# A fused two-stage network on one core: block 1's attention and scan woven into its projections, heads in pairs

## What is computed

```python
u = rmsnorm(x, ln1_g)
q, k, v, pool_in, z, xbc, dt_raw, gate_pre = split(u @ w_in)
y_a = dilated_attention_mixer(q, k, v, rel_bias) @ w_a   # 3 groups of 6 heads, 64 features, dilation 1, 4, 16
y_b = pool_mixer(pool_in, pool_w, pool_scale) @ w_b      # windows 2, 4, 8, 16
y_c = ssd_mixer(z, xbc, dt_raw, ...) @ w_c               # conv + silu, scan in 4 chunks of 128, gate by silu(z), norm
g = sigmoid(gate_pre + b_gate)
x = x + (g[0] * y_a + g[1] * y_b + g[2] * y_c) @ w_o
x = x + conv_ffn(rmsnorm(x, ln2_g), ...)
```

## Time and profile before

| | |
|---|---|
| Median of 3 runs | 3329.92 us (3324.21 to 3331.27) |
| The profiled execution | 3329.93 us, span 3328.1 us |
| PE busy | 3144.7 us (94%), 13268 instructions |
| PE weight loads | 2424.1 us |
| DVE busy | 1571.3 us (47%) |
| ACT busy | 1248.2 us (38%) |
| Granted PE clock, mean | 0.956 of 2.4 GHz |
| Transfers | 259.04 MB, mean 78 GB/s |

### The profile page before, as it was taken

How to read it: one execution, slowest core, us unless ns; L and a number is a source line. 1 busy time by engine, 2 the same in 40 slices (tenths; PEclk the granted TensorE clock), 3 DMA queues, 4 the chain that set the end, 5 groups by cost and what they waited for, 6 DMA issues and landing times. The chain is left out here.

```text
span 3328.1 us, 36122 instructions
## 1 busy us (share of the span) xinstructions
PE 3144.7 (94%) x13268; PEld 2424.1 (73%) x13268; DVE 1571.3 (47%) x2141; ACT 1248.2 (38%) x1848; POOL 392.7 (12%) x233
## 2 busy tenths in 40 slices
PE   7888899979999999889999999999989999999998
PEld 6777678747777877556667788888656667788887
DVE  3323463664376466654553354143654554354241
ACT  3323232414254244454444343133554453342231
POOL 4000000000000000101111122222101111122221
PEclk9677899989999999999999999999999999999999
DMA  6111233202232333212222233333212222233332
GB/s 171 39 51 50 59 88 84 83 1 70 83 107 85 100 94 95 57 32 64 70 71 70 70 95 99 97 95 109 62 39 64 70 71 70 76 95 98 98 95 89
DMA packets 460161, 259.04 MB, mean 78 GB/s; under 512 B 20202, under 2 KB 452172, under 8 KB 460016
## 3 DMA queue, kind: packets, MB, share of 16 engines
q1 hardware_dynamic: 454064, 246.03, 25.6%
q0 software_dynamic: 5952, 11.13, 1.2%
HBM read 254.98 MB, written 5.64 MB: 78 GB/s over the span
## 5 line engine op out<-in xcount | busy, mean ns | idle before, releaser
L657 ACT ACTIVATE wH<-wR 128x1024 fp32r<-128x1024 f32 (+1 forms) x476 | 491.3, 1032 | 494.7 <-DMA wR<-in_w_mlp_out_dram 197.5
L662 DVE TENSOR_TENSOR wL<-wR,wH 128x1024 fp32r<-128x1024 f32 (+1 forms) x332 | 395.9, 1193 | 582.6 <-ACT wH L657 570.8
L693 POOL TENSOR_TENSOR wL<-wR,wH 128x1024 fp32r<-128x1024 f32 (+1 forms) x144 | 346.0, 2403 | 2002.1 <-ACT wH L657 2002.1
L712 PE MATMUL ps<-uH,wH 128*128 128x512 f32 x1224 | 485.3, 396 | 15.7 <-DVE wL L662 12.7
L712 PE MATMUL ps<-uL,wH 128*128 128x512 f32 x1224 | 480.0, 392 | 0.0
L712 PE MATMUL ps<-uH,wL 128*128 128x512 f32 x1224 | 479.5, 392 | 0.0
L724 PE MATMUL ps<-uH,wH 128*128 128x512 f32 x928 | 381.7, 411 | 5.0 <-DVE wL L662 3.6
L724 PE MATMUL ps<-uL,wH 128*128 128x512 f32 x928 | 379.5, 409 | 0.0
L724 PE MATMUL ps<-uH,wL 128*128 128x512 f32 x928 | 376.6, 406 | 0.0
L712 PEld LDWEIGHTS ps<-uH,wH 128*128 128x128 f32 x1224 | 232.3, 190 | 74.1 <-DVE wL L662 22.6
L712 PE MATMUL ps<-mH,wH 128*128 128x512 f32 x688 | 267.9, 389 | 2.1 <-DVE wL L662 2.1
(11 more groups left out here) (441 smaller groups left out, 4476.4 us busy)
## 6 DMA issues: line engine op xcount, KB each, us to landing
wR<-in_w_in_dram SPq DMA_DIRECT2D x185, 512.0 KB, 3.7
wR<-in_w_mlp_in_dram SPq DMA_DIRECT2D x64, 512.0 KB, 4.0
wR<-in_w_mlp_out_dram SPq DMA_DIRECT2D x64, 512.0 KB, 4.0
wR<-in_ffn_w_up_dram SPq DMA_DIRECT2D x44, 512.0 KB, 3.7
wR<-in_w_branch_dram SPq DMA_DIRECT2D x24, 512.0 KB, 3.4
wR<-in_w_out_dram SPq DMA_DIRECT2D x16, 512.0 KB, 4.1
wR<-in_ffn_w_down_dram SPq DMA_DIRECT2D x16, 384.0 KB, 3.3
wR<-in_ffn_w_down_dram SPq DMA_DIRECT2D x16, 320.0 KB, 3.0
```

The source lines that it names most:

```text
L657: st.f(st.e.activation(wH[:, slot, 0:n], wR[:, slot, 0:n], ACT.Copy), hi_ready, c + 1)
L662: st.f(st.e.tensor_tensor(wL[:, slot, 0:n], wR[:, slot, 0:n], wH[:, slot, 0:n].bitcast(F32), ALU.subtract), lo_ready, c + 1 if done is Non ...
L693: e.tensor_tensor(wL[:, slot, 0:n], wR[:, slot, 0:n], wH[:, slot, 0:n].bitcast(F32), ALU.subtract).then_inc(sem("lo_pool"), 1)
L712: ins = pe.matmul(outp, w[:, k, c0:c0 + m], x[:, k0 + k, :], start=k0 == 0 and s == 0, stop=k0 + kt == kn and s == len(steps) - 1)
```

## The change

Block 1 is rebuilt in the manner of the later layers. The order becomes: the setup and group 0's projections as before; attention over 9 pairs of heads, with 96 thirds between its steps (group 1, group 2, dt, the 12 tiles of xbc, in the order 8 to 11, then 0 to 7); the scan, with the 36 thirds of merge 0 between its steps; z, then the pool input; merge 2; pool weights; merge 1; output projection.

```diff
+def attn_steps(score, turned, value, logs, vturn, dtturn, alpha, fill):
+    for u in range(10):
+        if u < 9:
+            score(u, 0)
+            fill(2 if u < 3 or u > 5 else 3)
+        if u < 3:
+            score(u, 1)
+            fill(2)
+        if u == 6:
+            vturn()
+        if u == 0:
+            fill(6)
+            continue
+        turned(u - 1, 0)
+        fill(2 if u < 9 else 3)
+        turned(u - 1, 1)
+        fill(1 if 5 < u < 9 else 2)
+        value(u - 1)
+        if u in (4, 7):
+            logs(u // 3 - 1)
+        if u == 8:
+            dtturn()
+        fill(2)
+    logs(2)
+    fill(6)
+    for m in range(3):
+        alpha(m)
+        fill(2 if m < 2 else 1)
+def ssd_steps(bturn, xturn, decay, seg, pair, yturn, fill):
...
+    for n in range(18):
+        if n < 16:
+            if n % 4 == 0:
+                decay(n // 4)
+            seg(n)
+        fill(1)
+        if n >= 2 and n % 2 == 0:
+            pair((n - 2) // 4, (n - 2) % 4 // 2)
+        if n >= 5 and n % 4 == 1:
+            yturn((n - 5) // 4)
+        fill(1 if n < 11 else 0)
...
         def _(pe):
             setup_pe(pe)
-            attn_pe(pe)
-            rest(merge_pe(pe, 0, 3, 3, bH, bL))
-            pool_pe(pe)
-            rest(merge_pe(pe, 1, KD, 11, bH, bL))
-            ssd_pe(pe)
-            rest(merge_pe(pe, 2, KD, 19, bH, bL))
+            first_pe(pe)
+            fill = Fill(chain(qkv_pe(pe, 1), qkv_pe(pe, 2), dt_pe(pe), xbc_pe(pe), merge_pe(pe, 0, 3, 3, baH, baL)))
+            attn_pe(pe, fill.take)
+            ssd_pe(pe, fill.take)
+            z_pe(pe)
+            rest(merge_pe(pe, 2, KD, 11, yH, yL))
+            pw_pe(pe)
+            rest(merge_pe(pe, 1, KD, 19, pbH, pbL))
```

Two heads are handled as a pair `m` = 0, 1. Their scores use rows 0 to 63 and 64 to 127 of the array, and the value product now has v as weights and writes the two heads to two halves of the partitions, feature-major, so that the turns of the outputs go. The division by the sum moves ahead of the turn, eight operations of 128 or 256 columns for a pair:

```diff
+                    for m in range(2):
+                        ins = pe.matmul(o[HD * m:HD * m + HD, n * P:(n + 1) * P],
+                                        vt[g % 2][:, kt, (2 * t + m) * HD:(2 * t + m + 1) * HD], pT[:, m, x * P:(x + 1) * P],
+                                        start=y == 0, stop=y == len(mine) - 1)
...
+                for n in range(4):
+                    x = scores_at(v)[:, m, n * w + (P if g == 0 and n == 0 else 0):(n + 1) * w]
+                    st.s(e.tensor_scalar(x, x, stat[:, g, 2, n, h:h + 1], None, ALU.mult))
```

More of the change, by code:

```diff
@@ new lines, in qkv_pe, with first_pe @@
+    def qkv_pe(pe, g, first=0):
+        for j in range(first, 6 if g < 2 else 9):
+            slot = use(pe, ("qkv", g, j))
+            yield from product_thirds(pe, G("qkv", g, j), slot, uH, uL)
+        if g < 2:
+            yield from vtok_pe(pe, g)
+    def first_pe(pe):
+        product_pair(pe, [G("qkv", 0, t) for t in range(2)], [use(pe, ("qkv", 0, t)) for t in range(2)], KD, P, uH, uL, u_tile(0))
+        parts = qkv_pe(pe, 0, 2)
+        for _ in range(2 * THIRDS):
+            next(parts)
+        params_pe(pe)
+        rest(parts)
@@ new lines, in attn_act, with qkv_dve @@
+        for m in range(3):
+            follow("al", m)
+            e.wait_ge(sem("comb_ready"), m + 1)
+            st.w()
+            st.f(e.activation(baH[:, m, :], mg[:, m, :], ACT.Copy), sem("bH_ready"), m + 1)
+    def qkv_dve(st, g):
+        for j in range(6 if g < 2 else 9):
+            low(st, ("qkv", g, j))
+            if g == 0 and j == 3:
+                params_dve(st)
+            if g == 0 and j == 5:
+                params_lam_dve(st)
+            yield
+        for j in range(4 if g < 2 else 0):
+            low(st, ("vtok", g, j))
+            yield
@@ L1898, in build, with dt_act @@
-    ysq = at("ysq", [P, 4, S], F32, WK + 12 * 2048)
-    def ssd_act(st):
+        h, lo = wk(wH, slot, KD, 16), wk(wL, slot, KD, 16)
+        for s in range(3 * KD):
+            k, (w, x) = s // 3, ((h, uH), (h, uL), (lo, uH))[s % 3]
+            ins = pe.matmul(o[0:16, :], w[:, k, :], x[:, k, :], start=s == 0, stop=s == 3 * KD - 1)
+            if s == 3 * KD - 1:
+                g.close(ins)
+            if s % THIRD == THIRD - 1:
+                yield
+    def dt_act(st):
+        g = G("dt")
+        o = g.take(st.e)
+        st.w()
+        g.done(st, st.e.activation(dtf[:, :], o[0:16, :], ACT.Copy))
+        st.w()
+        st.e.sem_inc(sem("dtf_ready"), 1)
+        high(st, ("dt",))
+        yield
@@ L1901, in ssd_act, with dt_dve, dt_exp_act @@
+    def dt_dve(st):
+        low(st, ("dt",))
+        yield
+    def dt_exp_act(st):
         e = st.e
@@ L2054, in spread, with ssd_dve @@
+    def ssd_dve(st, follow):
+        e = st.e
+        dt = dts[:, 5]
         def spread(n):
@@ new lines, in z_pe, with norm @@
+    def z_pe(pe):
+        def norm(x):
+            pe.wait_ge(sem("ysq_taken"), 4 * x + 4)
+            g = M("yn", x)
+            o = g.open(pe)
+            g.close(pe.matmul(o[:, :], C("ones"), ytot[:, x, :], start=True, stop=True))
+        for kind in ("z", "pin"):
+            for m in range(8):
+                slot = use(pe, (kind, m))
+                g = G(kind, m)
+                o = g.open(pe)
+                g.close(product(pe, o[:, :], slot, KD, P, 0, P, uH, uL))
+                if (kind, m) == ("z", 5):
+                    norm(0)
+                if (kind, m) == ("pin", 1):
+                    norm(1)
@@ new lines, in pw_sp, with pw_pe @@
+    def pw_sp(e):
+        rows = a["pool_w"][0].rearrange("g r n -> (g r) n")
+        for x in range(2):
+            load(e, ("pw", x), by_k(rows, 4, 2 * P, 0, x * 4 * P))
+    def pw_pe(pe):
+        for m in range(KD):
+            if m % 4 == 0:
+                slot = use(pe, ("pw", m // 4))
+            g = G("pw", m)
+            o = g.open(pe)
+            x = 2 * (m // 2)
+            pe.wait_ge(sem("d_ready"), x + 2)
+            g.close(product(pe, o[:, :], slot, 2, 2 * P, (m % 2) * P, P, dH[:, x:x + 2, :], dL[:, x:x + 2, :],
+                            off=(m // 2 % 2) * 4 * P))
```

1542 lines of the change are left out of this document (821 added, 721 removed).

## The result

| | before | after |
|---|---|---|
| Median | 3330.60 us, 4 runs (3324.21 to 3333.81) | 3172.14 us, 4 runs (3171.39 to 3173.37) |
| Ratio | | 0.9527, 95% interval 0.951 to 0.9543 |
| Profiled execution, its span | 3329.93 us, 3328.1 us | 3172.14 us, 3170.2 us |
| Granted PE clock, mean | 0.956 | 0.981 |
| First attention step to the output projection | 819.60 us | 663.91 us |

The kernel is 158 us faster, 4.7%. The forecast of 3158 us is 14 us too low, and the range (3130 to 3205) holds the time. Nearly all of the gain comes from the stretch of the prediction: 819.60 - 663.91 = 155.7 us, where 171.9 were forecast. The output projection begins at 744.92 instead of 901.80. DVE's busy time in the stretch has not changed; PE's share went from 89% to 94% and its granted clock from 0.86 to 0.96.

What follows compares the result with a forecast made beforehand. TensorE (PE) was taken as the bound, slowed by waits and half clock. Work of 603.3 us plus losses of 44.4 made the stretch 647.7 instead of 819.60, 171.9 less, so 3158 us, range 3130 to 3205.

Steps and rivals of the forecast that it cites:

- The bound and its cure: First block's attention to output projection: PE bound, with idle waits and half clock; interleaving saves 171.9 of 819.60 us.
- (a): Attention score and value groups: each changes the array's division, 0.40 us for each of 21 groups, 8.4 us lost.
- (b): Attention steps 6 to 8: DVE filled, 15.6 us against PE's 16.0, no slack; 5 us lost, 0 to 9.
- (c): Alphas: two convolved tiles in DVE's queue keep the largest wait at 9.1, with lag 10; 5 to 14; 2 behind.
- (d): Scan with merge 0: PE 6.4 us per decay step against DVE's some 4.6; 5 us lost, 0 to 15.
- (e): z, pool input, pool weights, last merge: a few hand-overs and the last merge's end; 7 us lost, 3 to 12.
- (f): Half clock behind the stalls: short dips cost about half of what they last; 6 us lost, 0 to 20.
- Hand-overs set the pace: Interleaved stretch: DVE or ACT-DVE hand-overs set the pace, with stalls in steps 6 to 9; 3185 to 3240, chance 0.17.
- Slower than before: Half clock stays through the whole interleaved stretch, 288 us more, 3445 us; chance 0.02.
- The signs named beforehand: Projection near 730, alpha wait 7 to 13, other named waits under 5, attention clock above 0.95, DVE above 90%.
- signs of being wrong: Attention stages below a clock of 0.8, fills waiting for weights' low halves, or scan with merge 0 over 125 us.

Runs made afterwards that it cites:

- the lumped run: Changed kernel with the projections of steps 0 to 9 in three lumps instead of between the attention products: 3248.7 us, 0.9757.
- the copies first: Changed kernel with ScalarE copying both turned probability tiles out of PSUM before the fills' work in every attention step: 3177.5 us, 0.9543.
- the best run: Changed kernel, queues reordered: ACT's fill work before exponentials, alphas' chain without convolved tiles, step 9's own ACT order, logarithms together in step 8: 3156.4 us, 0.9479.
- tile and alphas together: Changed kernel with one tile's ACT work ahead of exponentials, no convolved tiles in the alphas' chain, dt's logarithm behind their exponentials: 3162.6 us, 0.9507.
- the run with GpSimd alone: Changed kernel with every second low half, from the dt product to the first block's last merge, made on GpSimd instead of VectorE: 3168.7 us, 0.9526.

## Why the prediction was right, and where not

**The bound and its cure: right.** PE was bound by idle pieces and the half clock they bring. With projections between the steps the first six steps lose 6.7 us where 7.0 were forecast, and the lumped run gives 77 us back.

**(a) Right.** A score group of two heads takes 1.09 us for 512 columns, the 24 matmuls behind it 5.58 instead of 5.44, the 16 behind a value group 3.85 where 3.75 stand behind a turn: 0.35 a group, 0.40 forecast. The value pairs do overlap, 1.02 us in group 1, which only the changed kernel could show. The Trainium skill ("TensorEngine Tiling (Array Packing)", Key Properties) has the drain between modes; these rows put its price, with the columns' own overhead, at a third of a us for both changes.

**(b) Near in DVE's work, wrong in what costs, and too small.** DVE's 15.7 us in step 7 and 17.5 in step 8 stand beside the 15.6 forecast (step 6 carries the dt product and has only 9.8). But the step counted each engine's work and left out that the two in-order queues wait for each other. The stage lost 22.8 us, not 7.4. ACT's queue kept the value products waiting 11.0 us in steps 7 and 8 and the first turns of step 6 waiting 3.6, and with less work on DVE the value products' wait stayed (9.7 for 11.2).

**(c) Right in its place, mis-sized.** The alpha wait is the largest, as forecast, with the two tiles in the chain. It is 14.9 us instead of 9 to 10, above the bounds of 5 to 14, and the stage lost 20.8 us instead of 12. DVE's queue of the changed kernel:

```profile
298.59 2.32 DVE L1978 SCALAR_TENSOR_TENSOR cvt<-ps,PT,cvt 128x511 f32<-128x511 f32 x3 [1.43 <-ACTq L1961]
...
303.06 1.05 DVE L1741 COPY lT<-ps 6x512 f32<-6x512 f32 x1
...
308.21 2.32 DVE L1978 SCALAR_TENSOR_TENSOR cvt<-ps,PT,cvt 128x511 f32<-128x511 f32 x3 [0.22 <-DVE lT L1774]
...
317.37 0.67 DVE L1779 TENSOR_TENSOR lx<-lT 6x512 f32<-6x512 f32 x1
```

From the copy at 303.06 to the last row operation, 324.04, the chain takes 21.0 us, and 20.0 were forecast. What the step left out is one more convolved tile, ahead of the copy: it began at 298.59, after 1.43 us of waiting for ACT, which had a table load and the logarithm of dt first (295.89 to 297.45). PE's turn began at 297.78, so DVE took it up 5 us late.

**(d) Right within its bounds, twice its estimate** (9.8 lost, of it 7.2 idle; 5 forecast, 0 to 15), and the scan with merge 0 took 125.4 us where the text set 125 as the mark. **(e) Too high:** 1.2 us lost, not 7; the end of the last merge, 4.0 before, waits for nothing.

**(f) Too low.** 663.9 - 627.0 = 36.9 us are idle; of the 24 above the work that are not, the mode changes have 7 (21 groups at 0.35), and about 17 are left for the half clock, where 6 stood. The step took the clock's price as half of "short dips". Against the 6.66 us at full clock, 5.2 us were lost right behind the wait of 14.9 us and 4.2 behind that of 6.2.

**The rivals.** *Hand-overs set the pace*, 3185 to 3240: the mechanism was there, in steps 6 to 9 alone, at 15 us where the rival had 15 to 30 more and a slow stretch besides. *Slower than before*: the clock is 1.00, 1.00, 0.90, 0.71, 0.99 in the five stages; all but the alphas are where the argument from the later layers (0.93 and 1.00) had them.

**The signs named beforehand.** The alpha wait is the largest and the waits before the turns of probabilities are under 5 us, as said. The others missed: the output projection begins at 744.92, not near 730; the alpha wait is over 13; the spread tiles' waits are 5.5 in total; the clock of steps 6 to 9 is under 0.95; DVE is busy 43, 72 and 66% in steps 6 to 8, not over 90; the dt product takes 3.71 us for 16 matmuls and 3.14 for the last 8, which run at half clock, not 5.4. Two signs of being wrong appeared, narrowly or in one place: the scan's 125.4 us, and the clock of 0.71 in the alphas. The stretch lost 17 us more than forecast: 24 more in the stages of (b) and (c) and 5 in that of (d), less 6 of (e) and the 6 that (f) had set aside. The range's upper end, 47 us above the forecast, left room for that.

## What to carry to other kernels

When two engines feed each other in order, write the two queues side by side and look at what stands behind each wait: a piece of work that is ready and stands behind a wait is lost on both. Moving one instruction to where it is wanted only moved the wait (the copies first, no faster). Filling the time in which the engine waits anyway, together with a clear chain to the alphas and an order of its own for step 9, gave 16 us. A step without the usual work (the last of a pipelined loop) needs its own order. And when work moves to another engine, look whether the engine that it left has really become less busy: here it had not.

## What the runs showed of the hardware

How much a wait costs in clock depends on more than its length. Before the first alpha products PE waited 14.9, 6.2 and, in the best run, 4.7 us, and the same work behind it (6.66 us at full clock) took 11.90, 10.90 and 11.06 (305.88 to 316.94). Where a wait of 14.4 us stood before projection matmuls instead (tile and alphas together, until 310.45), the first eight took 3.71 us and the three alpha products behind them 2.89, where they took 5.41 in the other three. Behind the waits of 3.6, 3.6 and 7.4 us in steps 6 to 8 the clock was low for 4.3, 3.8 and 5.2 us. In the best run the value product took 1.02 us where nothing was waited for and 1.91 behind a wait of 2.7. The clock can also fall with no wait just before: behind the second three alpha products, 16 matmuls took 5.32 us in the changed kernel (338.95 to 344.27) and 3.89 in the best run. Steps 3 to 5, which have no wait, ran at 1.00 throughout. Why it falls in some of these places and not in others, the runs don't show.

While GpSimd makes a low half (2.4 us), a DVE operation on two SBUF tiles waits for it. In the run with GpSimd alone, seven such operations begin while one is being made, at 248.38, 270.98, 287.95, 300.89, 336.16, 374.84 and 416.01. They last 1.18 to 2.77 us, where 0.68 or 0.69 is usual, and each ends about 0.55 us behind GpSimd's. Operations that read PSUM kept their time (L1981 at 231.13, three in 2.32 us).

A table load takes 1.28 us, and ACT's next instruction begins within 0.02 us of its end (245.13 to 246.43). The Trainium skill ("ScalarE: Activation LUTs", What ACT_TABLE_LOAD costs) has 1283 ns for the load, as measured here, but also some 1380 ns of drain with every switch of sets, 2.66 us in all; here the instruction before the load ends at 245.03 and the one behind it begins at 246.43, 1.40 us later. Between tanh and the exponentials of the next step there is no load. The Trainium skill's section on table sets has exp and tanh in one set, and the rows agree.
